# Bias sums one attention unit further forward in GpSimd's order, in a hybrid decoder layer

## The reference

```python
score = jnp.where(key_pos[None, None, :] <= t[None, :, None], score, NEG_INF)
_, sel = lax.top_k(score, topk)                       # topk = 128
bias = bias_tab[t5_bucket(t - sel)]                   # relative position, per head
logits = einsum('bqhd,bqkd->bhqk', qb, kg) * scale + bias
p = masked_softmax(logits, (dist >= 0)[:, None])
return einsum('bhqk,bqkhd->bqhd', p, vg)
```

## Time and profile before

| | us |
|---|---|
| median of 3 runs | 637.4 |
| lowest and highest | 635.86, 637.65 |
| time of the profiled execution | 635.86 |
| its span, first to last instruction | 633.8 |
| TensorE busy | 571.4 (90%) |
| VectorE, ScalarE, GpSimd busy | 381.9, 330.5, 221.2 |

### The profile page before, as it was taken

How to read it: one execution, slowest core, us unless ns; L and a number is a source line. 1 busy time by engine, 2 the same in 40 slices (tenths; PEclk the granted TensorE clock), 3 DMA queues, 4 the chain that set the end, 5 groups by cost and what they waited for, 6 DMA issues and landing times.

```text
span 633.8 us, 10756 instructions
## 1 busy us (share of the span) xinstructions
PE 571.4 (90%) x4131; PEld 326.2 (51%) x4131; DVE 381.9 (60%) x901; ACT 330.5 (52%) x579; POOL 221.2 (35%) x164
## 2 busy tenths in 40 slices
PE   3999989698999999689899899976899998899997
PEld 2545655344346855356566476634556555333443
DVE  6512386625589998887877746435546676576311
ACT  4645654427446776451822615674667776244410
POOL 0163642512015383342441620435431233142520
PEclk9999999989599899799999989999999999899999
DMA  9347855523002431220220210212031211072311
GB/s 316 113 108 175 136 121 178 166 83 101 1 20 67 133 101 57 77 67 2 68 68 1 68 34 3 69 33 68 1 99 35 68 67 67 3 261 69 133 51 50
DMA packets 31171, 52.88 MB, mean 83 GB/s; under 512 B 2743, under 2 KB 13329, under 8 KB 31121
## 3 DMA queue, kind: packets, MB, share of 16 engines
q1 hardware_dynamic: 30825, 51.68, 28.2%
q10 hardware_dynamic: 296, 0.52, 0.5%
HBM read 49.77 MB, written 2.42 MB: 82 GB/s over the span
## 4 chain that ended last, share of the span: by engine, by line
PE 66%; DVE 18%; ACT 6%; issue 5%; POOL 3%; SPq 2%; DMA 1%; DVEq 0%; ACTq 0%; POOLq 0%
PE bank L1585 12%; PE bank L1587 11%; PE bank L1586 11%; PE bank L1857 4%; PE bank L1861 4%; PE bank L1859 4%; PE bank L1768 4%; PE bank L1776 3%; PE bank L1748 2%; PE bank L1621 2%; DVE work L1291 2%; DVE early L1196 2%; POOL w_lo L512 2%; ACT stage L718 2%; DVE small L1193 1%
## 5 line engine op out<-in xcount | busy, mean ns | idle before, releaser
L512 POOL TENSOR_TENSOR w_lo<-stage,w_hi 128x1024 f16<-128x1024 f32 (+4 forms) x76 | 149.4, 1968 | 225.1 <-ACT w_hi L726 225.1
L726 ACT ACTIVATE w_hi<-stage 128x1024 f16<-128x1024 f32 (+4 forms) x76 | 74.5, 981 | 12.8 <-issue 8.9
L1857 PE MATMUL bank<-hT_hi,w_hi 128*128 128x512 f16 x192 | 74.3, 387 | 1.7 <-PE bank L1861 0.9
L1859 PE MATMUL bank<-hT_lo,w_hi 128*128 128x512 f16 x192 | 73.9, 385 | 0.5 <-PE bank L1587 0.5
L1861 PE MATMUL bank<-hT_hi,w_lo 128*128 128x512 f16 x192 | 73.8, 385 | 0.3
L718 ACT ACTIVATE stage<-stage,small 128x512 f32<-128x512 f32 (+4 forms) x120 | 73.6, 662 | 0.5 <-DMA stage<-in_w_in 0.4
L1585 PE MATMUL bank<-w_hi,hT_hi 128*128 128x260 f16 (+4 forms) x192 | 61.7, 321 | 2.7 <-DVE hT_lo L997 1.4
L1586 PE MATMUL bank<-w_lo,hT_hi 128*128 128x260 f16 (+4 forms) x192 | 61.5, 320 | 0.0
L1587 PE MATMUL bank<-w_hi,hT_lo 128*128 128x260 f16 (+4 forms) x192 | 61.5, 320 | 0.0
L1776 PEld LDWEIGHTS bank<-work 64*64 64x64 f32 x992 | 37.1, 139 | 30.6 <-DVEq L1263 21.0
L1776 PE MATMUL bank<-work 64*64 64x64 f32 x992 | 43.6, 227 | 10.1 <-DVEq L1263 9.5
(11 more groups left out here) (319 smaller groups left out, 1166.1 us busy)
## 6 DMA issues: line engine op xcount, KB each, us to landing
stage<-in_w_in SPq DMA_DIRECT2D x40, 512.0 KB, 3.6
stage<-in_c_phi_w SPq DMA_DIRECT2D x8, 512.0 KB, 4.4
stage<-in_w_branch SPq DMA_DIRECT2D x8, 512.0 KB, 3.7
stage<-in_w_out SPq DMA_DIRECT2D x8, 512.0 KB, 4.5
stage<-in_w_in SPq DMA_DIRECT2D x8, 260.0 KB, 2.8
strips<-rel_rows SPq DMA_DIRECT2D x8, 256.0 KB, 7.3
late<-in_x SPq DMA_DIRECT2D x1, 2048.0 KB, 9.1
out_x<-late SPq DMA_DIRECT2D x8, 256.0 KB, 2.0
```

Source lines behind the costliest of these rows:

```text
L512: gp.tensor_tensor(piece_view(w_lo[:, k % PAIRS, :], c), piece_view(stage[:, piece_at[c, j] % STAGES, :], c), piece_view(w_hi[:, k % PAIRS ...
L726: nc.scalar.activation(piece_view(w_hi[:, k % PAIRS, :], c), full, ACT.Copy).then_inc(hi_ready, 1)
L1857: mm(G.bank(g)[:, :], w[0], h[0], start=k == 0, stop=False)
L1859: mm(G.bank(g)[:, :], w[0], h[1], start=False, stop=False)
```

## The change

In GpSimd's loop the join for unit u+2 in iteration u becomes the join for unit u+3, from iteration 3 on instead of 4. The twelve joins keep their order and their waits; what moves is their place against `lo_split` and `gate_z`. Every other engine's list is unchanged.

```diff
             join(4)
             join(5)
             for u in range(len(units)):
-                if u >= 4 and u + 2 < 16:
-                    join(u + 2)
+                if u >= 3 and u + 3 < 16:
+                    join(u + 3)
                 for c, j in attention_splits(u):
                     lo_split(c, j)
                 if u % 4 == 3 and u >= 7:
```

## The result

| | before | changed |
|---|---|---|
| median, us | 637.65 (5 runs) | 631.38 (5 runs) |
| lowest and highest | 635.86, 640.04 | 627.92, 634.02 |
| profiled execution, time and span | 635.86, 633.8 | 631.91, 629.9 |

The ratio is 0.989, 95% interval 0.985 to 0.994: 1.1% faster, some 7 us of 637.65 with an interval of 4 to 10. The prediction was 630.0 in a range of 626.4 to 633.5.

The account below looks back on a forecast made before the run. TensorE, busy 90% of 633.8 us, was held by late GpSimd joins through VectorE. Terms -1.96 - 3.08 + 0.95 - 1.7 + 1.1 - 1.95 = -6.6 us gave 629.3 or 630.8; 630.0 was taken, range 626.4 to 633.5.

Parts of the forecast that it names:

- term 5: Four VectorE subtractions meeting split, gating and joins 11 and 12: GpSimd loses time, join 11 later; +1.1 us, bounds 0 and 2.1.
- Term 4: With TensorE's wait near unit 10 shortened, the granted clock stays up instead of falling: -1.7 us.
- Term 1: Unit 6: join 6 passes the split of iteration 3, so logits 6 start with their products: -1.96 us.
- Term 2: Unit 10: join 10 passes split and gating, so TensorE's wait of 2.92 us goes: -3.08 us.
- term 3: Join 11, behind split and gating, is late next; low half 9 follows late and TensorE idles: +0.95 us.
- full case of 2.1: Term 5's upper bound: GpSimd never yields, subtractions wait until join 12 ends, logits 11 2.1 us late; rival's chance 0.14.
- 4 to 6: Sign expected: VectorE's 13.2 us of waiting for GpSimd's sums (L666) falls to 4 to 6.
- Term 6: Unit 14: join 14 passes the gating of iteration 11; TensorE's 2.42 us of waits shrink to 0.47: -1.95 us.
- the third wait: TensorE's idling of 1.10 us before 453.36, behind late logits 14; claimed to cause the later 0.52 and 0.80.
- No split later: GpSimd's splits: the join can start before the split's high half is complete, so no cost is taken.
- The gain reaches the end: From unit 16 on, later waits are released by work that moves along; rival that nothing reaches the end: 0.05.

Follow-up runs that it names:

- join 6: Only join 6 moved ahead of the split of iteration 3, against the kernel before: stretch 38.35 us, median 634.48, ratio 1.000.
- join 14: Only join 14 moved ahead of the gating of group 1, against the kernel before: stretch 38.81 us, median 636.81, ratio 1.002.
- join 10: Only join 10 moved ahead of the split of iteration 7 and the gating, against the kernel before: stretch 38.12 us, median 635.39, ratio 0.999.
- first comparison: The changed kernel's first timing against the kernel before: median 631.38 us (5 runs), ratio 0.989 (0.985 to 0.994).
- the second: The changed kernel timed again against the kernel before, on one chip with two other kernels: median 631.64 us (12 runs), ratio 0.994 (0.990 to 0.997).
- subtractions in iteration 4: The changed kernel with VectorE's four subtractions (L1491) in iteration 4 instead of 8: stretch 33.75 us, 630.53 us (1 run).
- join u+4 with the subtractions in iteration 12: Join u+4 in iteration u and the subtractions in iteration 12, against the kernel before: 629.52 us, ratio 0.986; again 630.64, 0.993.
- joins 6 and 10: Joins 6 and 10 moved, join 14 not, against the kernel before: stretch 36.09 us, median 631.19 (12 runs), ratio 0.994.

## Why the prediction was right

The forecast of -6.6 us in this place came out as -6.41 in the trace, and the time fell within the range in both comparisons (631.38, 631.64). The waits were the ones named and went as described; one mechanism (term 5) was wrong with a nearly right size, which is luck, and one term (4) held in its place but not in the time. Step by step, with the 2.50 us of the later start taken off:

- *Term 1, unit 6 (-1.96).* Transposes 7 at 430.90 instead of 432.89: -1.99. Logits 6 at 424.86 (424.85 forecast), logits 7 at 428.52 (428.5 forecast), held by join 7 in the place that join 6 had.
- *Term 2, unit 10 (-3.08).* `unit_out` 8 at 436.43 instead of 441.50, 5.07 early (5.04 forecast).
- *Terms 3 and 5, the wait of join 11 and the subtractions (+0.95, +1.1).* TensorE waited 2.00 us (2.05 forecast). The 0.74 left without the subtractions is term 3, less than 0.95; term 5 is 1.26, more than 1.1, and the two errors cancel. Term 5 came by another way than the one chosen: I let GpSimd lose 1.1 us to them, and it lost 0.1 (0.78 + 2.32 for what takes 0.72 + 2.25). VectorE lost: 3.40 us for 1.1, one subtraction for each GpSimd instruction that had to end first. The full case of 2.1 was too pessimistic, since one subtraction got through behind each of them and only the last waited for join 12. By the same waits VectorE's 13.2 us for L666 fell to 3.1 and not to 4 to 6: ahead of logits 11 it was held in the subtractions instead.
- *Term 4, the clock (-1.7).* 1.00 throughout the stretch; with one join each it fell at the wait of 2.93 us (joins 6 and 14) and stayed up behind 2.01 (join 10). But over whole executions the changed kernel loses no less to the clock than the kernel before (24.5 and 24.1 us), so in the time this term isn't found (its 1.7 is narrowly outside the interval). The 1.7 is an estimate from one row, 4 us x (1 - 0.57); the three traces with a fall in this place (before, join 6, join 14) each have 3.4 us at 0.50 there, 1.71 us of cycles. Only one execution of the kernel before has a trace, so how often its fall comes isn't known.
- *Term 6, unit 14 (-1.95).* Singly 1.85; in the full change -5.07 + 2.00 - 1.7 leaves 1.64 of the 6.41 for it. Transposes 15 came without a wait; the 0.80 before transposes 16 stayed whole, in all twelve profiles, where I had let the three shrink to 0.47. So it didn't stem from the third wait, as the prediction has it.
- *No split later (0).* The split of iteration 3 began 0.07 us behind its high half (428.04, high half from 426.91 for 1.06), and that of iteration 7 0.08 (436.72, from 435.58 for 1.06), as before (0.07 and 0.08).
- *The gain reaches the end.* In the profiled pair 173.62 against 173.61. In time 7 us (4 to 10) by the first comparison and 4 (2 to 6) by the second. At full clock the second has 4.9 us, as the stretch without its 1.7 of clock; what is missing of the 6.4 is about term 4.

What held it together was that each term was read off a place where one engine was idle and another named, and that all four timelines were carried forward unit by unit; the one wrong turn was who yields to whom. The old trace had the answer in the starts of the single subtractions (first, then the other three):

```profile
L1491 DVE TENSOR_TENSOR v_c<-raw_c,v_c x1: 1115/1115/1115, 441.3 to 441.3; 128x128 f16<-128x128 f32 x1
...
L1491 DVE TENSOR_TENSOR v_c<-raw_c,v_c x3: 278/279/279, 442.3 to 442.7; 128x128 f16<-128x128 f32 x3
```

GpSimd's chain of joins ended at 442.24 (438.98 + 3.26). The first subtraction waited for that end; the three of 279 ns ran when GpSimd stood idle. The median was no sign that subtractions beside a join are mostly cheap: the only one that had a join beside it cost the join's remainder.

## What to carry to other kernels

- In an engine with a strict order, a small result that another engine needs soon belongs ahead of a large one that is waited for; it may go as far forward as its own wait ends before the large one's. Compare the two waits in the code: here both hung on the same `logits(u+1)`, and the split started no later (0.07 us behind its high half, as before).
- When a wait goes, look at what stands between it and the next on the same engine. Here four small subtractions, 1.72 us from first to last before, grew to 3.40 when they met a chain of GpSimd instructions.
- Where a row gives shortest, median and longest, ask for the instructions one by one before taking the median: here it came from those that ran when the neighbour was idle.
- Measure such a change by the distance between two marks in the trace, on either side of it. The stretch repeated to 0.02 us where times scatter by 1%. It tells what the change does in its place; what the clock makes of it elsewhere needs the timed runs.

## What the runs showed of the hardware

VectorE's four subtractions (L1491), which read both inputs from SBUF, were held while a GpSimd instruction ran (a sum, a gating or a split, all reading SBUF), and one got through behind each: in nine cases out of nine, in four kernels (before, changed, subtractions in iteration 4 and in 12), a subtraction that took 390 to 1347 ns, against 278 with GpSimd idle, ended 0.1 to 0.2 us behind such an end. Four in a row took 1.14 us with a join beside the first alone, and 2.67 or 3.40 beside three or four GpSimd instructions. These lost about 0.1 us in all (two joins took 1.78 us instead of 1.72, the gating and two joins 3.10 instead of 2.97). No semaphore stands between the subtractions and these instructions, and the profile counts the held time as VectorE's busy time. So "only through semaphores", as the opening has it, doesn't hold for these cases.

The granted clock fell at a wait of TensorE of 2.92 or 2.93 us in three profiles of three, behind 1.99 to 2.01 in none of four, behind the 2.25 before transposes 2 in none of twelve, and yet behind a wait of 1.70 us in five of twelve and one of 1.49 in eight. So the length of one wait doesn't decide it, and the same code meets it differently. Each of these 16 falls was 3.4 us at 0.50, that is 1.71 us of cycles; it began between 0.6 us ahead of the wait's end (join 6 alone, at 442.7) and 1.2 us behind it. In the part behind the stretch one cost 1.7 or 1.2 us. Over whole runs the mean granted clock differs between kernels by more than chance (0.958 for join u+4 with the subtractions in iteration 12 and 0.964 for joins 6 and 10, over 12 runs each).
